# Two decoder layers on one core: shared-gate steps dealt out among the router's, splitting of x and the scaled input taken off TensorE, an own room for pair 0's first quarter, and the way between the layers in halves

## What is computed

```python
for l in range(2):
    mix = _token_mixer(x, ...)                       # ends in o @ w_out
    x = _layer_norm(ALPHA * x + mix, ln1_g[l], ln1_b[l])
    ffn = _moe(x, ...)
    x = _layer_norm(ALPHA * x + ffn, ln2_g[l], ln2_b[l])

def _moe(x, ...):
    s = sigmoid(xt @ w_router)                       # 256 x 64
    # group-limited top 8 of 64 by s + b_router; gw = s of the chosen, normalised, times 2.5
    routed = sum over the chosen experts e: gw * ((silu(xt @ w_gate[e]) * (xt @ w_up[e])) @ w_down[e])
    shared = (silu(xt @ ws_gate) * (xt @ ws_up)) @ ws_down
    return routed + shared
```

## Time and profile before

| | us |
|---|---|
| median of 3 runs | 1251.35 (1250.69 to 1252.87) |
| the profiled execution | 1250.69 |
| its span, first to last instruction | 1249.1 |
| TensorE busy | 1217.4 (97%) |
| VectorE, ScalarE, GpSimd busy | 551.7, 336.7, 134.5 |
| mean granted TensorE clock | 0.995 of full speed |
| read from HBM | 452.26 MB, 363 GB/s over the span |

### The profile page before, as it was taken

How to read it: one execution, slowest core, us unless ns; L and a number is a source line. 1 busy time by engine, 2 the same in 40 slices (tenths; PEclk the granted TensorE clock), 3 DMA queues, 4 the chain that set the end, 5 groups by cost and what they waited for, 6 DMA issues and landing times.

```text
span 1249.1 us, 25165 instructions
## 1 busy us (share of the span) xinstructions
PE 1217.4 (97%) x10424; PEld 632.8 (51%) x10426; DVE 551.7 (44%) x1537; ACT 336.7 (27%) x692; POOL 134.5 (11%) x181
## 2 busy tenths in 40 slices
PE   9998999999999999999899989999999999999995
PEld 7885854433444343443389858433433444443341
DVE  5788463333333333333358875533333333333334
ACT  4657321111111111111256573111111111111111
POOL 2661220000000000000035523000000000000000
PEclk9999999999999999999999999999999999999998
DMA  9544689999999999999845538899999999999994
GB/s 356 175 182 189 269 353 427 424 428 426 426 425 427 425 427 426 425 427 425 350 171 203 197 142 356 354 425 427 426 427 426 427 424 428 425 427 426 425 427 192
DMA packets 41849, 454.87 MB, mean 364 GB/s; under 512 B 4881, under 2 KB 5649, under 8 KB 7441
## 3 DMA queue, kind: packets, MB, share of 16 engines
q1 hardware_dynamic: 41456, 452.27, 87.1%
q10 hardware_dynamic: 288, 1.05, 0.2%
HBM read 452.26 MB, written 1.05 MB: 363 GB/s over the span
## 4 chain that ended last, share of the span: by engine, by line
PE 83%; DVE 6%; DMA 5%; ACT 4%; issue 1%; DVEq 0%; ACTq 0%; POOL 0%; POOLq 0%
PE banks L1003 33%; PE banks L1023 17%; PE banks L984 7%; PE banks L1034 5%; DMA expert_weights<-in_moe_w 5%; PE banks L933 2%; ACT prob L1252 2%; PE banks L1011 1%; PE banks L873 1%; PE banks L875 1%; PE banks L874 1%; PE banks L779 1%; PE banks L601 1%; PE banks L569 1%; PE banks L965 1%
## 5 line engine op out<-in xcount | busy, mean ns | idle before, releaser
L1003 PE MATMUL banks<-expert_weights,gathered 128*64 128x512 f32 x1536 | 343.3, 595 | 1.9 <-DMA expert_weights<-in_moe_w 1.9
L1003 PEld LDWEIGHTS banks<-expert_weights,gathered 128*64 128x64 f32 x1536 | 105.8, 137 | 234.4 <-issue 229.0
L1023 PE MATMUL banks<-expert_weights,hT 128*32 128x512 f32 x1600 | 182.0, 595 | 2.2 <-DVE gathered L1775 1.1
L1789 DVE TENSOR_TENSOR sig<-sig,banks 128x256 f32<-128x256 f32 x64 | 26.9, 421 | 338.5 <-ACT sig L1348 338.2
L1361 ACT ACTIVATE y_hi<-banks,gate_slot 128x512 fp32r<-128x512 f32 x126 | 86.6, 687 | 294.8 <-PE banks L1023 294.8
L1799 DVE SCALAR_TENSOR_TENSOR y_lo<-banks,gate_slot,y_hi 128x512 fp32r<-128x512 f32 x126 | 94.7, 751 | 157.2 <-ACT y_hi L1361 157.2
L1348 ACT ACTIVATE sig<-banks 128x256 f32<-128x256 f32 x64 | 24.5, 383 | 410.9 <-PE banks L1003 410.9
L984 PEld LDWEIGHTS banks<-hot,x_part 128*128 128x128 bf16 x3072 | 93.2, 98 | 50.0 <-issue 50.0
L1023 PEld LDWEIGHTS banks<-expert_weights,hT 128*32 128x32 f32 x1600 | 47.1, 109 | 109.4 <-issue 106.4
L984 PE MATMUL banks<-hot,x_part 128*128 128x64 bf16 x3072 | 100.6, 193 | 0.0
L1414 POOL TENSOR_TENSOR piece_lo<-piece,piece_hi 128x256 fp32r<-128x256 f32 x112 | 88.0, 821 | 82.1 <-ACT piece_hi L1194 66.8
(11 more groups left out here) (236 smaller groups left out, 1536.6 us busy)
## 6 DMA issues: line engine op xcount, KB each, us to landing
expert_weights<-in_moe_w SPq DMA_DIRECT2D x134, 2048.0 KB, 23.9
expert_weights_in_ring<-in_moe_w SPq DMA_DIRECT2D x20, 2048.0 KB, 24.0
piece<-in_pieces SPq DMA_DIRECT2D x32, 1024.0 KB, 5.1
expert_weights<-in_moe_w SPq DMA_DIRECT2D x24, 1024.0 KB, 9.5
expert_weights_in_rows<-in_moe_w SPq DMA_DIRECT2D x22, 1024.0 KB, 23.1
expert_weights_in_x<-in_moe_w SPq DMA_DIRECT2D x22, 1024.0 KB, 24.0
expert_weights_in_ring<-in_moe_w SPq DMA_DIRECT2D x8, 1024.0 KB, 9.3
shared_weights<-in_ws SPq DMA_DIRECT2D x2, 3072.0 KB, 12.5
```

Source lines behind the costliest of these rows:

```text
L1003: mm = pe.matmul(C[e * PAIR:(e + 1) * PAIR, :], xgT[:, d, e * PAIR:(e + 1) * PAIR], w[:, e, part], start=(d == 0), stop=(d == KD - 1))
L1023: mm = pe.matmul((A, B)[c][to:to + SLOTS, :], hT[:, f, of_:of_ + SLOTS], W[QUARTERS + c][:, e, f * 512:(f + 1) * 512], start=(f == 0), sto ...
```

## The change

1. **Gates dealt out.** The 32 steps of the shared gate are taken one by one (`gates_on`): 5 behind tile 0's scores, 1 between the two halves of turning tile 1, 19 behind tile 1's scores, 7 behind the ranks. Turning and copying of tile 1 go by halves of 512 columns, its normalisation's last step too (`ln_half`); the scores start on the first half.
2. **x parts and scaled input.** Tile 0's two subtractions go from GpSimd to VectorE, ahead of tile 1's normalisation; tile 1's stay on GpSimd, in halves. `add_input` and the scaled identity are gone: ScalarE writes ALPHA times x into banks 0 to 3 (`residual`), tile 0 early and tile 1 behind the split; TensorE waits for them in pair 1, SP before it loads over x.
3. **Own room for pair 0's first quarter.** It is loaded, 0.5 MB per expert, to where y_hi and y_lo come later (`first_quarter`), behind the third and the fourth part of the output projection; the half room that it leaves takes the first half of load 8 (`ROOMS`) before the loop. y_lo, the second tile's rest and two parts of x change their places.
4. **Waits of the loop.** `xg` becomes two semaphores: `gate_up` waits for ScalarE's half at d = 0 and for VectorE's at d = 4; `down` waits for both. The first `gate_up` waits for the shared gate (bank 6 is in use until then).
5. **Between the layers.** ScalarE takes a root of a constant ahead of time, which loads its table; statistics, variance, centring and stretching go by tile and by half (`ln_first`), tile 0 whole before tile 1's last statistics; TensorE turns by halves; the first piece is asked for behind the last `gate_up`. The last layer's end stays.

```diff
-IN_TWO = [k for k in range(LOADS * PAIRS) if room_of(k) == LAST_ROOM or k in (3, 8, 9, 10, 11, 12, 13, LOADS * PAIRS - 1)]
+IN_TWO = [k for k in range(LOADS * PAIRS) if room_of(k) == LAST_ROOM or k in (0, 3, 8, 9, 10, 11, 12, 13, LOADS * PAIRS - 1)]
...
+        xg_at = moe_at[0]
         xgT = place("gathered", [P, KD, P], F32, where=moe_at)
-        xs0 = [None] + [place(f"x_part{j}_0", [P, D], BF16, where=moe_at) for j in range(1, 3)]
+        y_lo_at = moe_at[0]
+        y_lo = place("y_lo", [P, D], F32R, where=moe_at)
...
+        first_quarter = [place(f"first_quarter_expert{e}", [P, EW // CHUNKS], F32, where=[(moe_at[0], y_lo_at)[e]]) for e in range(2)]
         y_hi = place("y_hi", [P, D], F32R, where=moe_at)
-        y_lo = place("y_lo", [P, D], F32R, where=moe_at)
...
-        residual_in = sem("residual_in_banks", 1)
+        first_ld = sem("first_quarter_loaded", 32)
+        residual_in = sem("residual_in_banks", 2 * TT)
...
             before = range(k + 1)
+            if k == c == 0:
+                return first_ld, 32
             if c == 0:
+                before = range(1, k + 1)
                 return room_ld[room_of(k)], 16 * sum(room_of(m) == room_of(k) for m in before)
...
+def load_first_quarter(e):
+    cols = slice(e * EW // CHUNKS, (e + 1) * EW // CHUNKS)
+    sp.dma_start(first_quarter[e][:, :], of(moe_w)[0, 0, 0, :, cols]).then_inc(first_ld, 16)
...
-for k in range(LOADS):
+load_half(0, 1)
+for k in range(1, LOADS):
     load(k)
+load_half(ROOMS, 0)
...
+load_first_quarter(0)
 load_half(3, 1)
 load(4)
 sp.wait_ge(*at(mix, 2 * TT))
+load_first_quarter(1)
 load(5)
 load(6)
 for t in range(TT):
     normalised(sp, 0, t)
 load_half(7, 0)
-sp.wait_ge(*at(split_rest, TT))
-sp.wait_ge(*at(residual_in, 1))
+sp.wait_ge(*at(split_rest, TT + 1))
+sp.wait_ge(*at(residual_in, 2 * TT))
 load_half(7, 1)
-for k in range(ROOMS, LOADS * PAIRS):
+sp.wait_ge(*at(*used(0, 1)))
+load_half(ROOMS, 1)
+for k in range(ROOMS + 1, LOADS * PAIRS):
...
-        sp.wait_ge(*at(combined, 2 * TT))
+        sp.wait_ge(*at(main.gu, QUARTERS * PAIRS))
         for g in range(2):
             load_first(layer + 1, 0, g)
+        sp.wait_ge(*at(combined, 2 * TT))
...
+        pe.wait_ge(*at(ln_first, t + 1, 1))
+        turn_x_half(pe, t, 0, bank[4 + 2 * t])
+    def turn_second(t):
         normalised(pe, 1, t, 1)
-        turn_x(pe, t, (bank[4 + 2 * t], bank[5 + 2 * t]))
+        turn_x_half(pe, t, 1, bank[5 + 2 * t])
     pe.wait_ge(*at(ln_var, TT + 1, 1))
-    keep_clock(10)
-    turn_normalised(0)
+    keep_clock(8)
+    turn_first(0)
+    keep_clock(3)
+    turn_second(0)
     for g in range(2):
         pe.wait_ge(*at(first_piece[g], 16))
     pe.wait_ge(*at(xt_sb, 5, 1))
     project_first(0, 0)
-    turn_normalised(1)
     pe.wait_ge(*at(xt_sb, 6, 1))
     project_first(0, 1)
+    turn_first(1)
+    turn_second(1)
...
-def turn_tile(t):
-    normalised(pe, 0, t)
-    turn_x(pe, t, (bank[4 - 2 * t], bank[5 - 2 * t]))
-def add_input(t, c):
-    return pe.matmul(bank[2 * t + c][:, :], alpha_i[:, :], x_sb[:, t, c * 512:(c + 1) * 512], start=True, stop=False, skip_group_check=True)
 def score_tile(t):
-    pe.wait_ge(*at(xt_sb, 2 * t + 2))
     for k in range(KD):
+        if k % 4 == 0:
+            pe.wait_ge(*at(xt_sb, 2 * t + k // 4 + 1))
         mm = pe.matmul(bank[5][:, t * NE:(t + 1) * NE], xT[:, k, t * P:(t + 1) * P], wr[:, k, :], start=(k == 0), stop=(k == KD - 1))
     mm.then_inc(logits, 1)
...
                        xT[:, k, t * P:(t + 1) * P], start=(k == 0), stop=(k == KD - 1))
     return mm
-def shared_gate(f, t, ks=range(KD)):
-    return shared_gate_up(f, t, bank[6][:, (f * TT + t) * P:(f * TT + t + 1) * P], ks)
+gate_steps = [(f, t, k) for t in range(TT) for f in range(2) for k in range(KD)]
+def gates_on(count):
+    for _ in range(count):
+        f, t, k = gate_steps.pop(0)
+        mm = shared_gate_up(f, t, bank[6][:, (f * TT + t) * P:(f * TT + t + 1) * P], (k,))
+    return mm
 pe.wait_ge(*at(wr_ld, 16))
 pe.wait_ge(*at(ws_ld, 16))
-turn_tile(0)
-pe.wait_ge(*at(alpha_ready, 1))
-add_input(0, 0)
+normalised(pe, 0, 0)
+turn_x(pe, 0, (bank[4], bank[6]))
 score_tile(0)
-shared_gate(0, 0)
-shared_gate(1, 0, range(KD // 2))
-turn_tile(1)
-shared_gate(1, 0, range(KD // 2, KD))
+gates_on(5)
+pe.wait_ge(*at(ln_half, 1))
+turn_x_half(pe, 1, 0, bank[4])
+gates_on(1)
+normalised(pe, 0, 1)
+turn_x_half(pe, 1, 1, bank[7])
 score_tile(1)
-shared_gate(0, 1)
-shared_gate(1, 1).then_inc(sh_ps, 1)
-add_input(0, 1)
+gates_on(19)
 A, B, C, R = bank[4], bank[5], bank[6], bank[7]
 pe.wait_ge(*at(sel_ready, 1))
 chosen = slb[:, :, :].rearrange("p t e -> p (t e)")
 pe.matmul(A[:, 0:TT * NE], upperb[:, :], chosen, start=True, stop=True).then_inc(ranks, 1)
 pe.matmul(R[0:1, T:T + TT * NE], upperb[:, P - 1:P], chosen, start=True, stop=True).then_inc(ranks, 1)
-add_input(1, 0)
+gates_on(len(gate_steps)).then_inc(sh_ps, 1)
...
-    pe.wait_ge(*at(sw.xg, 2 * k))
     each = KD // QUARTERS
     for d in range(KD):
+        if d % 4 == 0:
+            pe.wait_ge(*at((sw.xg_act, sw.xg_dve)[d // 4], k))
...
+    if first:
+        W[0] = [w[:, :] for w in first_quarter]
     loaded = [landed(LOADS * n + j // 2, j % 2) for j in range(CHUNKS)]
+    if first:
+        pe.wait_ge(*at(sh_gate, 1))
     gate_up(main, W, n + 1, loaded)
...
+    if n == 1:
+        pe.wait_ge(*at(residual_in, 2 * TT))
...
-        pe.wait_ge(*at(main.xg, 2 * (n + 2)))
+        pe.wait_ge(*at(main.xg_act, n + 2))
+        pe.wait_ge(*at(main.xg_dve, n + 2))
...
-add_input(1, 1).then_inc(residual_in, 1)
...
+    act.activation(ln_s[:, 0, 22:23], own_number[:, 0:1], ACT.Sqrt)
     act.wait_ge(*at(main.dn, 2 * PAIRS, 1))
-    deviation(3, (0, 1), 1)
+    deviation(3, (0,), 1)
     split_hi(2)
+    copy_xT(act, 4, 0, (bank[4], bank[5]), 1)
+    deviation(4, (1,), 1)
     split_hi(3)
-    for t in range(TT):
-        copy_xT(act, 4, t, (bank[4 + 2 * t], bank[5 + 2 * t]), 1)
+    copy_xT(act, 4, 1, (bank[6], bank[7]), 1)
...
-def split_x(t):
-    normalised(act, 0, t)
-    act.wait_ge(*at(mix, 2 * TT - 1 + t))
-    act.copy(xs[0][t][:, :], x_sb[:, t, :]).then_inc(split_a, 1)
+halves = (slice(0, 512), slice(512, D))
+def split_x(t, cols):
+    act.copy(xs[0][t][:, cols], x_sb[:, t, cols]).then_inc(split_a, 1)
+def residual(t):
+    for c in range(2):
+        act.activation(bank[2 * t + c][:, :], x_sb[:, t, halves[c]], ACT.Copy, scale=ALPHA).then_inc(residual_in, 1)
 def router_out(t):
     act.wait_ge(*at(logits, t + 1))
     act.activation(rt[:, 0, t, :], bank[5][:, t * NE:(t + 1) * NE], ACT.Sigmoid).then_inc(lg_exp, 1)
-def split_again(t):
-    if t == 0:
-        act.wait_ge(*at(mix, 2 * TT))
-    act.wait_ge(*at(split_rest, t + 1))
-    act.copy(xs[1][t][:, :], rest[t][:, :]).then_inc(split_b, 1)
+def split_again(t, cols, count):
+    act.wait_ge(*at(split_rest, count))
+    act.copy(xs[1][t][:, cols], rest[t][:, cols]).then_inc(split_b, 1)
+def copy_x_half(g, from_):
+    act.wait_ge(*at(xt_ps, 2 + g + 1))
+    act.copy(xT[:, 4 * g:4 * g + 4, P:2 * P], from_.rearrange("p (k c) -> p k c", k=4)).then_inc(xt_sb, 1)
 deviation(1, (0,))
-split_x(0)
-copy_xT(act, 0, 0, (bank[4], bank[5]))
-split_again(0)
+normalised(act, 0, 0)
+split_x(0, slice(0, D))
+residual(0)
+act.wait_ge(*at(mix, 2 * TT - 1))
+split_again(0, slice(0, D), 1)
+copy_xT(act, 0, 0, (bank[4], bank[6]))
 deviation(2, (1,))
 router_out(0)
-split_x(1)
-copy_xT(act, 0, 1, (bank[2], bank[3]))
+act.wait_ge(*at(ln_half, 1))
+split_x(1, halves[0])
+copy_x_half(0, bank[4])
+copy_x_half(1, bank[7])
+normalised(act, 0, 1)
+split_x(1, halves[1])
+split_again(1, halves[0], 2)
 router_out(1)
-split_again(1)
+split_again(1, halves[1], 3)
+residual(1)
...
+x_rest(1, quarters[0:2], 2)
+x_rest(1, quarters[2:4], 3)
+x_last(1, quarters[0:2], 2)
+x_last(1, quarters[2:4], 3)
...
+deviations(0, (0,))
+stretch(0, whole)
 V.tensor_copy(upperb[:, :], upper[:, 0, 0:P])
 for par in range(2):
     own.mark(V.tensor_copy(gwp[par][:, TT * 6:SLOT_COLS], own_number))
+dve.wait_ge(*at(split_a, 1))
+V.tensor_tensor(rest[0][:, :], x_sb[:, 0, :], xs[0][0][:, :], ALU.subtract).then_inc(split_rest, 1)
+dve.wait_ge(*at(mix, 2 * TT - 1))
+add_sublayer(1, 0, mixed_out(1, 0))
+dve.wait_ge(*at(split_b, 1))
+V.tensor_tensor(xs[2][0][:, :], rest[0][:, :], xs[1][0][:, :], ALU.subtract).then_inc(split_c, 1)
+dve.wait_ge(*at(mix, 2 * TT))
+add_sublayer(1, 1, mixed_out(1, 1))
+deviations(0, (1,))
+stretch(1, halves[0], ln_half)
+stretch(1, halves[1])
...
+if layer == DEPTH - 1:
+    for c in range(2):
+        for t in range(TT):
+            statistics(c, t)
+    deviations(1, (0, 1))
+    stretch(0, whole)
+    for cols in halves:
+        centre(1, 1, cols)
+        stretch(1, cols)
+else:
+    statistics(0, 0)
+    statistics(0, 1)
     for t in range(TT):
-        dve.wait_ge(*at(combined, c * TT + t + 1))
-        own.mark(V.bn_stats(ln_s[:, t, c * 6:c * 6 + 6], bank[2 * t + c]))
-deviations(1, (0, 1))
-stretch(0, whole)
```

(8 more changed lines are left out.)

84 lines of the change are left out of this document (44 added, 40 removed).

## The result

The changed kernel takes 1244.16 us (median of 4 runs, 1242.28 to 1244.48), the kernel before 1252.11 beside it (4 runs, 1250.69 to 1253.34): a ratio of 0.994, 95% interval 0.9925 to 0.9954. So it is faster by 0.6%, some 7.9 us. The profiled execution took 1243.99 with a span of 1242.2, against 1250.69 and 1249.1: 6.9 us of span are there to be explained, where the sum said 9.0.

The account below looks back on a forecast made before the run. TensorE and DMA were read as a dead heat in the long loops, with DMA ending layer 0's. Savings of 3.3 + 2.4 + 3.3 = 9.0 us gave 1241.7 profiled, a median of 1242.3; range 1239.5 to 1247.0.

Parts of the forecast that it names:

- the sum: Whole kernel: 3.3 us for each layer's loop and 2.4 between the layers, 9.0 us saved in all.
- The 1.4: End of layer 0's loop before the change: TensorE alone would have come 1.4 us earlier, at 607.2.
- The way into the loop, 2.5: Stretch before the first gate_up, walked in layer 0's times: gate_up starts at 166.4, 2.5 us earlier; bounds 1.4 and 3.7.
- The loop's end, 3.3: End of each layer's loop: 3.5 us earlier at 605.0, taken as 3.3 per layer; bounds 2.4 and 3.9.
- The going of the gap: Way into layer 0's loop: the DMA standstill at 168 to 170, share 0.02, goes as loads are issued earlier.
- Rival 1: DMA or VectorE holds more back: loops end 2.4 earlier, between layers gives 1.0; 5.8 in all, 1245.5 us; chance 0.16.
- Between the layers, 2.4: From layer 0's end to layer 1's project(1): project(1) starts at 633.5, 2.4 us earlier; bounds 1.0 and 2.9.
- The table's share: Between the layers: the 1.28 us table load held VectorE only about 0.5 us, since centring ran beside it.
- Rival 3: New waits bring a granted clock of 0.50: two dips cost 3.4 us, 1245.7 us; chance 0.10.
- Rival 4: Loop: extra waits for gathered input, 0.2 us per pair, cost 12.4 against 9.0, 1254.8 us; chance 0.03.
- Rival 2: TensorE leads everywhere: 3.9 + 2.9 + 3.9 = 10.7 us saved, 1240.6 us; chance 0.06.
- Rival 5: No change: gains lost to unseen waits, such as the first quarter landing behind 166.4; 1251 us; chance 0.03.

Follow-up runs that it names:

- first pair delayed: Changed kernel plus four products of zeros, some 0.9 us, ahead of each layer's first gate_up; 1247.32 us, ratio 0.9968.
- own room undone: Changed kernel with pair 0's first quarter back in its old place in room 0; 1244.53 us, ratio 0.9949.
- between undone: Changed kernel with statistics, stretches, table load and first-piece request between the layers as in the kernel before; 1248.03 us, ratio 0.9969.

## Why the prediction was right, and where its sum was off

**What bounds it.** Right: DMA ends the loop, and TensorE alone would be through 1.0 to 1.3 us sooner, shown by the MB left out. The 1.4 that the prediction read for the kernel before fits the 1.5 and 1.4 worked out above.

**The way into the loop, 2.5.** Measured 2.00 and 1.97. Nearly every link came as walked: turned halves at 155.38 (155.4), router of tile 1 done at 158.54 (158.6), selection ended at 163.08 (162.9). The missing 0.5: 0.13 of the shift was there before the entry and is no gain of it; the ranks began at 163.19 instead of 162.9, since TensorE follows the last selected bits by some 0.1 and these were 0.2 later; the gates took 1.66 for 1.6 and the gathering 1.59 for 1.5. The shared gate, called "as late as the gathering", was: with zeros put in front of the first pair, TensorE waited 0.24 for it.

**The loop's end, 3.3.** This is the term that was too large: 2.51 and 2.13 measured, counted from the same points, 0.5 beyond the entry in layer 0 and 0.16 in layer 1. Two things went wrong in it. First, load 10's release came 2.0 earlier and not 2.5 (its first half is issued at 179.28, before at 181.26), just as the entry did: that is 0.5 of the 0.8 too much in layer 0. Second, the 3.5 set a computed end against a measured one. The sum 178.6 + 1.4 + 425 = 605.0 has its twin for the kernel before, 181.1 + 1.4 + 425 = 607.5, and that kernel's last gate_up was measured at 608.6. Like for like the forecast release moves the end by 2.5, the entry and no more, which the prediction had as its lower bound (2.4, DMA moves with the rooms only); the other 1.0 was a loss that its sum doesn't hold, counted as a gain. The going of the gap was to give what lay beyond the entry, 0.8; it is gone, but the rate behind it is 361 GB/s and not 401, and 0.5 and 0.16 were left. A wait of 0.91 and 1.03 stayed where 0.3 was forecast. Rival 1 had the loops at 2.4 each: in the loops it was right, between the layers (1.0) it was not.

**Between the layers, 2.4.** Measured 1.93, in its bounds. Counted from the last gate_up, the first product came 2.36 earlier (16.96 for 19.32) where the walk had 2.6, and from there to project(1) it takes 8.29 us where the walk had 8.2 and the old form 7.86. The table's share was 1.03, not 0.5, so that the halves and the new order gave 0.9 where the forecast's 2.4 left 1.9 for them: two errors that partly cancel, which is luck. The centring, which had covered most of the table load before, is in halves now and covers half as much, so with halves the early table is worth more than the rows of before could say.

**Rivals 2 to 5.** Rival 3 (the clock) is real in kind: a low clock stood between the layers in three of the fourteen profiles, once behind the old form's waits and twice behind the unexplained stop, but not in the changed kernel's own. Rival 4 falls: from 200 to 600 us TensorE is busy for 399.98, and no wait for gathered input is among its ten largest. Rival 2 falls with the wait of 0.9 to 1.0 for weights: TensorE led nowhere in the loop. Rival 5 falls with the time.

**The sum.** 2.51 + 1.93 + 2.13, with 0.13 and 0.20 outside, is 6.9 for 9.0: 2.0 of the 2.1 missing lie in the loops' terms and 0.5 between the layers, less the 0.33 outside. Of the signs only one held in full: no DMA window from 147 to 600 under 0.8. The first gate_up came at 166.75 (166.4), in layer 1 6.5 earlier (8.2), project(1) 4.6 earlier (5.7), and the wait was 0.9 to 1.0 (0.3 or less). One sign of being wrong was there too: the loops take 439.2 and 439.4 us, more than the 438.3 that stood for TensorE alone. The time landed in the range, since every part gave its lower bound or came within 0.3 of it.

**Not tried apart.** No run undoes the two semaphores for the gathered input, the halves of tile 1 on the way in, or the earlier request for the first pieces by themselves; what each of them gives is open.

## What to carry to other kernels

Where two resources run a dead heat, take something off the way in for both: time gained ahead of the loop came out at its end (2.0 at the first gate_up, 2.5 and 2.1 at the last). When you forecast an end from a sum of rates, work out the same sum for the kernel before and compare the two sums; against a measured end the sum's own error counts as gain. Judge the DMA engines by the bytes that they moved over the whole way in, not by their busy share and not by one gap. A gap can have two causes of which each alone keeps most of it shut, so ask what issues each load before you price it. And hold back some small products that nobody waits for, to stand where TensorE would idle for another engine: with none behind the ranks it idled for 0.90 us.

## What the runs showed that I had not expected

- In layer 0's mixer a granted clock of 0.50, for about 3.4 us, stood either behind the first longer idle time, of 1.08 to 1.19 us (90 to 94; six profiles, the kernels before and after among them), or behind two shorter ones of 0.49 and 0.67 some 20 us later (109 to 113; four profiles, such as the one with the first pair delayed), or in neither place (own room undone, between undone), with the same program there. It costs 1.2 us by the transposes (150.52 against 149.29). The length of the first idle time doesn't tell the cases apart (1.14 to 1.19 in the six without a low clock behind it), but its end does: 88.82 to 89.39 us in the first six, 89.47 and 89.52 in the two without, 89.87 to 90.81 in the other four. So which case it is goes with when TensorE comes there in an execution; why was not tried. One profile before and after an edit can differ by this much for no reason that lies in the edit.
- TensorE stopped for 1.9 to 2.2 us in products that wait for nothing, in three of the four kernels with a longer program, and in no other.
- The DMA share stood at 0.85 to 0.94 with 279 to 336 GB/s moved, where in the steady stretch 1.01 goes with 426: a share of 0.91 (180 to 182) can go with two thirds of the bytes.
